# One encoder block on one Trainium2 core: 24 instead of 12 seven-product pairs in the down projection, weight sums made in the up projection

## What is computed

```python
n1 = rmsnorm(x, norm_mix_g)
proj = n1 @ w_in                      # 2048 -> 6152: mLSTM heads and RG-LRU blocks
x = x + mix @ w_out                   # 2048 x 2048
n2 = rmsnorm(x, norm_ffn_g)
gate, up = jnp.split(n2 @ w_up, 2, axis=-1)          # 2048 -> 2 x 5632
gate = causal_dwconv(gate, ffn_conv_w, ffn_conv_b)   # width 3
x = x + (jax.nn.silu(gate) * up) @ w_down            # 5632 -> 2048
return rmsnorm(x, norm_final_g)
```

## Time and profile before

| | |
|---|---|
| time, median of 3 runs | 1127.09 us (1127.08 to 1127.31) |
| span of the profiled execution | 1124.7 us; its own time is not listed apart from the three runs |
| busy: PE, weight loads | 1112.0 us (99%), 959.1 us (85%) |
| busy: DVE, ACT, POOL | 809.1 us (72%), 601.3 us (53%), 47.2 us (4%) |
| moved by DMA | 213.09 MB, mean 189 GB/s |
| mean granted TensorE clock | 0.997 of full speed |

### The profile page before, as it was taken

The page is one execution under the profiler, slowest core; times in us unless marked ns, Lnnn a source line. Parts: engine busy times, 40 slices in busy tenths (PEclk is TensorE's granted clock), DMA queues, the critical chain, the costliest instruction groups (busy, mean ns, idle before and its releaser), DMA issues.

```text
span 1124.7 us, 18049 instructions
## 1 busy us (share of the span) xinstructions
PE 1112.0 (99%) x5986; PEld 959.1 (85%) x5986; DVE 809.1 (72%) x1088; ACT 601.3 (53%) x818; POOL 47.2 (4%) x44
## 2 busy tenths in 40 slices
PE   9999999999999999999999999999999999999997
PEld 8888888888888888888888888888888888878886
DVE  6777586675775676776667667766766998689876
ACT  7656475564756554344444444444444666457553
POOL 0100000000000000000000000000000000000001
PEclk9999999999999999999999999999999999999999
DMA  8756657566565566656656665666566666556552
GB/s 256 234 166 192 178 147 231 151 186 186 198 202 173 175 198 190 185 172 211 196 168 187 206 189 164 207 199 191 158 214 191 221 228 219 170 168 217 196 183 78
DMA packets 166558, 213.09 MB, mean 189 GB/s; under 512 B 6988, under 2 KB 149584, under 8 KB 166400
## 3 DMA queue, kind: packets, MB, share of 16 engines
q1 hardware_dynamic: 165504, 210.40, 60.3%
q0 software_dynamic: 448, 1.78, 0.5%
q10 hardware_dynamic: 576, 0.53, 0.1%
HBM read 210.58 MB, written 2.10 MB: 189 GB/s over the span
## 4 chain that ended last, share of the span: by engine, by line
PE 95%; DVE 2%; ACT 1%; DMA 0%; issue 0%; DVEq 0%; ACTq 0%
PE ps L1305 42%; PE ps L1307 21%; PE ps L1440 21%; PE ps L1489 5%; PE ps L1302 2%; PE ps L1303 1%; PE ps L1288 1%; DVE w L721 1%; PE ps L1416 1%; ACT xn L411 0%; ACT w L411 0%; PE ps L1335 0%; DMA xres<-x_dram 0%; DVE xres L1038 0%; DVE s_w L1062 0%
## 5 line engine op out<-in xcount | busy, mean ns | idle before, releaser
L1305 PE MATMUL ps<-xT,w 128*128 128x512 f32 x2048 | 715.3, 395 | 0.0
L721 DVE TENSOR_TENSOR w<-raw,w 128x1024 fp32r<-128x1024 f32 x364 | 444.7, 1235 | 255.6 <-ACT w L411 254.8
L1307 PE MATMUL ps<-xT,w 128*128 128x256 f32 x2048 | 569.6, 278 | 0.0
L411 ACT ACTIVATE w<-raw 128x1024 fp32r<-128x1024 f32 (+2 forms) x373 | 384.8, 1045 | 336.7 <-PE ps L1307 242.1
L1305 PEld LDWEIGHTS ps<-xT,w 128*128 128x128 f32 x2048 | 384.1, 188 | 88.9
L1307 PEld LDWEIGHTS ps<-xT,w 128*128 128x128 f32 x2048 | 385.5, 188 | 0.3
L1440 PE MATMUL ps<-w,aT 128*128 128x512 f32 x1152 | 265.9, 391 | 2.5 <-DVE xres L1093 2.5
L1440 PEld LDWEIGHTS ps<-w,aT 128*128 128x128 f32 x1152 | 217.1, 189 | 48.0 <-DVE xres L1093 2.9
L411 ACT ACTIVATE fs<-fc 128x512 f32<-128x512 f32 x22 | 13.9, 632 | 101.4 <-DVE fc L1164 101.4
L1489 PE MATMUL ps<-s_w,s_act 128*128 128x512 f32 x252 | 59.2, 390 | 0.2 <-DVE xres L1038 0.2
L1489 PEld LDWEIGHTS ps<-s_w,s_act 128*128 128x128 f32 x252 | 47.2, 188 | 10.4 <-DVE xres L1038 0.7
(11 more groups left out here) (178 smaller groups left out, 577.5 us busy)
## 6 DMA issues: line engine op xcount, KB each, us to landing
raw<-w_up_dram SPq DMA_DIRECT2D x176, 512.0 KB, 4.6
raw<-w_in_dram SPq DMA_DIRECT2D x92, 512.0 KB, 3.9
raw<-w_down_dram SPq DMA_DIRECT2D x64, 512.0 KB, 4.4
raw<-w_out_dram SPq DMA_DIRECT2D x32, 512.0 KB, 4.5
s_raw<-w_down_dram SPq DMA_DIRECT2D x24, 512.0 KB, 4.9
raw<-w_in_dram SPq DMA_DIRECT2D x8, 256.0 KB, 7.0
xres<-x_dram SPq DMA_DIRECT2D x3, 512.0 KB, 7.3
y_dram<-xn SPq DMA_DIRECT2D x3, 384.0 KB, 3.2
```

The source lines that it names most:

```text
L411: return sc.activation(out_, in_, fn, **kw)
L721: v.tensor_tensor(w[:, s, :, 1, :], raw[:, s, :].rearrange("p (c n) -> p c n", c=CH), w[:, s, :, 0, :], ALU.subtract).then_inc(lo_ready, 1)
L1305: mm(full, w[:, s, c, 0, cut], xT[:, kt, :, :].rearrange("p a n -> p (a n)"), start=kt == 0, stop=False)
L1307: ins = mm(rest, w[:, s, c, 1, cut], xT[:, kt, 0, :], start=False, stop=kt == KT - 1)
```

## The change

Twelve pairs per half instead of six: four runs, each a body and three pairs, then one more body (five bodies instead of eight). The first and third pair of a run use `s_raw` and `s_w` (places `_x`), the second uses the ring's own `raw`, `w` and `aT`. The weight sums of all 24 pairs are made in the up projection: SP loads a pair's two K tiles (1 MB), DVE makes four sums in two steps between splits, SP stores them (1 MB) to device memory; the down projection loads them again. Activation tiles and their sums lie side by side, so a pair's activations are one operand of 896 columns. In half 0 the last body goes by slots. `pairs_out` is no longer spread over splits. `gfin` has lost its own buffer and is loaded into used slots of `act`.

```diff
-PERIODS = 6
-PERIOD = RING + 2
-DOWN_BODIES = (FT - 2 * PERIODS) // RING
+RUNS, RUN_PAIRS = 4, 3
+PAIRS = RUNS * RUN_PAIRS
...
+DOWN_BODIES = (FT - 2 * PAIRS) // RING
...
+SUMS_AT = (2, 8, 14, 20, 26, 32)
+SUMS_GAP = 6
...
+        pair_raw = s_raw[:], raw_flat
+        pair_w = s_w[:], w[:].rearrange("p s c a n -> p (s c a n)").rearrange("p (m a n) -> p m a n", m=S_WEIGHTS, a=2)
...
-                    sp.dma_start(s_raw[:, 2 * k:2 * k + 2, :].rearrange("p a n -> p (a n)"),
-                                 rows[bass.ds(b * PERIOD + (RING + k), 1), :, half * HALF:(half + 1) * HALF].rearrange("k p n -> p (k n)")).then_inc(s_landed, 16)
+                    src, dst = rows[:, bass.ds(first + s, 1), half * HALF:(half + 1) * HALF], raw[:, s, :].rearrange("p (b n) -> p b n", b=1)
+                    if pair_before is None:
+                        load(group, s, src, dst)
+                    else:
+                        sp.wait_ge(s_lo_ready, pair_before * S_PARTS + (1 if s < 2 else S_PARTS))
+                        sp.dma_start(dst, src).then_inc(raw_landed[s], 16)
...
+            def load_for_sums(run, q):
+                half, i = divmod(q, RUN_PAIRS)
+                src = down_rows[bass.ds(run * RUN_TILES + (RING + 2 * i), 2), :, half * HALF:(half + 1) * HALF]
+                sp.dma_start(s_raw[:, 0:2 * HALF].rearrange("p (k n) -> p k n", k=2), src.rearrange("k p n -> p k n")).then_inc(t_raw_landed, 16)
+            def store_sums(run, q):
+                t = run * len(SUMS_AT) + q
+                dst = sums_dram[bass.ds(t, 1)].rearrange("t p n -> p (t n)")
+                sp.wait_ge(t_summed, t * T_SUMS + T_SUMS)
+                sp.dma_start(dst, s_raw[:, 2 * HALF:4 * HALF]).then_inc(t_stored, 16)
...
+            def load_pair(half, run, i):
+                place, p = place_of(i), nth_pair(half, run, i)
+                cols = half * HALF
...
+                    sp.wait_ge(lo_ready, g * RING + (RING + 2))
+                elif i:
+                    sp.wait_ge(s_lo_ready, p * S_PARTS + (1 - 2 * S_PARTS))
+                elif half or not at_start(run):
+                    sp.wait_ge(s_lo_ready, p * S_PARTS + (1 - S_PARTS))
+                sp.dma_start(dst[:, 0:BANK], upper).then_inc(plain_landed[place], 16)
+                sp.dma_start(dst[:, BANK:BANK + HALF], lower).then_inc(plain_landed[place], 16)
+                if i == 1:
+                    sp.wait_ge(lo_ready, g * RING + 2 * RING)
+                elif i:
+                    sp.wait_ge(s_lo_ready, p * S_PARTS - S_PARTS)
+                elif half or not at_start(run):
+                    sp.wait_ge(s_lo_ready, p * S_PARTS)
+                sp.dma_start(dst[:, 2 * HALF:4 * HALF], sums).then_inc(sums_landed[place], 16)
             COL_Q, COL_K, COL_V, COL_O, COL_XR, COL_GR = 0, D_M, 2 * D_M, 3 * D_M, 4 * D_M + 2 * H, 4 * D_M + 2 * H + D_L
...
+                load_group(j * 2 + (G_UP + g), up_v, j * COLS + g * D_FF, ahead)
...
+            after(sp, A2, "std1")
+            with sp.Fori(0, RUNS) as run:
+                for it in range(RUN_ITERS):
+                    for g in range(2):
+                        def sums_of(s, unit=(2 * it + g) * RING):
+                            if unit + s - SUMS_GAP in SUMS_AT:
+                                store_sums(run, SUMS_AT.index(unit + s - SUMS_GAP))
+                            if unit + s in SUMS_AT:
+                                load_for_sums(run, SUMS_AT.index(unit + s))
+                        load_up(run * RUN_ITERS + (it + 1), g, sums_of)
+            for j in range(RUNS * RUN_ITERS + 1, UP_ITERS):
                 for g in range(2):
-                    load_group(j * 2 + (G_UP + g), up_v, j * COLS + g * D_FF)
+                    load_up(j, g)
...
+                load_pairs(half, 0)
+                with sp.Fori(1, RUNS) as run:
+                    load_body(run + g0, w_down, run * RUN_TILES, half, nth_pair(half, run, -2))
+                    load_pairs(half, run)
+                load_body(g0 + RUNS, w_down, RUNS * RUN_TILES, half, nth_pair(half, RUNS, -2))
+                for b in range(RUNS + 1, DOWN_BODIES):
                     load_body(g0 + b, w_down, FT + (b - DOWN_BODIES) * RING, half)
                 if half == 0:
-                    load_pair(1, 0)
                     load_body(g0 + DOWN_BODIES, w_down, 0, 1)
             for r in range(ROWS):
...
-            def prepare_body(src, group, first):
+            def prepare_body(src, group, first, pair_before=None):
                 for s in range(RING):
+                    if pair_before is not None:
+                        act_e.wait_ge(s_used, pair_before * S_STEPS + (1 if s < 2 else S_STEPS))
                     round_units(group, [s])
+                    if pair_before is not None:
+                        act_e.wait_ge(s_used, pair_before * S_STEPS + S_STEPS)
                     round_tiles(src, first, [s])
...
+                act_e.wait_ge(plain_landed[place], nth * S_LOADS + S_LOADS)
+                if i == 1:
+                    act_e.wait_ge(unit_used, g * RING + (RING + 2))
+                elif i:
+                    act_e.wait_ge(s_used, p * S_STEPS + (1 - 2 * S_STEPS))
+                elif half or not at_start(run):
+                    act_e.wait_ge(s_used, p * S_STEPS + (1 - S_STEPS))
...
+                if i == 1:
+                    act_e.wait_ge(unit_used, g * RING + 2 * RING)
+                elif i:
+                    act_e.wait_ge(s_used, p * S_STEPS - S_STEPS)
+                elif half or not at_start(run):
+                    act_e.wait_ge(s_used, p * S_STEPS)
+                act_fn(pair_act[place][:, 0, 0:A_COLS], pair_source(run, i)).then_inc(s_hi_ready, 1)
+                act_e.wait_ge(sums_landed[place], nth * 16 + 16)
+                for m in (T1, T2):
+                    act_fn(dst[:, m:m + 2, 0, :], src[:, m * BANK:(m + 2) * BANK].rearrange("p (m n) -> p m n", m=2)).then_inc(s_hi_ready, 1)
...
+                    def run_of_pairs(run):
+                        for i in range(RUN_PAIRS):
+                            pair_hi(half, run, i)
+                        if half == 1 and at_start(run):
+                            warm_sqrt(A4)
+                            for r in range(ROWS):
+                                squares(A4, r, 0, V4)
+                        prepare_body(act, run + (g0 + 1), run * RUN_SLOTS + RUN_SLOTS, nth_pair(half, run, RUN_PAIRS - 2))
+                    run_of_pairs(0)
+                    with act_e.Fori(1, RUNS) as run:
+                        run_of_pairs(run)
                     pairs_copy(half)
-                    prepare_body(act, g0 + DOWN_BODIES - 1, FT - RING)
+                    for b in range(RUNS + 1, DOWN_BODIES):
+                        prepare_body(act, g0 + b, ACT_SLOTS + (b - DOWN_BODIES) * RING)
                     if half == 0:
                         prepare_body(act, g0 + DOWN_BODIES, 0)
...
+                low(0, dst[:, 0:PLAIN, 1, :], src[:, 0:PLAIN * BANK].rearrange("p (m n) -> p m n", m=PLAIN), dst[:, 0:PLAIN, 0, :])
+                low(1, pair_act[place][:, 1, 0:A_COLS], pair_source(run, i), pair_act[place][:, 0, 0:A_COLS])
+                for n, m in ((2, T1), (3, T2)):
+                    low(n, dst[:, m:m + 2, 1, :], src[:, m * BANK:(m + 2) * BANK].rearrange("p (m n) -> p m n", m=2), dst[:, m:m + 2, 0, :])
...
-                did(v.tensor_tensor(xres[:, 0, first], bank_a, xres[:, 0, first], ALU.add), V4, f"xa{half}")
-                yield
-                did(v.tensor_tensor(total, bank_c, copy_a, ALU.add), V4, f"u{half}")
-                yield
+                did(v.tensor_tensor(xres[:, 1, second], bank_a, xres[:, 1, second], ALU.add), V4, f"xa{half}")
+                did(v.tensor_tensor(total, bank_c, total, ALU.add), V4, f"u{half}")
                 after(dve, V4, f"u{half}")
-                did(v.tensor_tensor(xres[:, 0, second], total, xres[:, 0, second], ALU.add), V4, f"xu{half}")
-                yield
+                did(v.tensor_tensor(xres[:, 1, first], total, xres[:, 1, first], ALU.add), V4, f"xu{half}")
                 did(v.tensor_tensor(total, bank_e, total, ALU.add), V4, f"z{half}")
-                yield
...
+                    def run_of_pairs(run):
+                        for i in range(RUN_PAIRS):
+                            pair_lo(half, run, i)
...
-                    split_body(act, g0 + 1, PERIOD, tiles + RING)
-                    with dve.Fori(1, PERIODS) as b:
-                        pair_lo(half, b)
-                        split_body(act, b + (g0 + 1), b * PERIOD + PERIOD, b * RING + (tiles + RING))
...
-                        split_units(g0 + DOWN_BODIES - 1, [s])
-                        split_tiles(act, FT - RING, tiles + (DOWN_BODIES - 1) * RING, [s])
-                        next(parts)
-                    for s in range(RING):
-                        if half == 0:
-                            split_units(g0 + DOWN_BODIES, [s])
```

(75 more changed lines are left out.)

208 lines of the change are left out of this document (97 added, 111 removed).

## The result

| | before | after |
|---|---|---|
| median of the runs | 1127.09 us | 1150.13 us (1147.57 to 1154.12) |
| ratio to before | | 1.021, 95% interval 1.0198 to 1.0222 |
| span of the profiled execution | 1124.7 us | 1145.7 us (its time 1147.57) |
| mean granted TensorE clock | 0.997 | 0.986 |
| matmuls on the two down lines | 1404 | 1368 |

What follows compares the result with a forecast made beforehand. TensorE was taken as the bound (busy 1112.0 of 1124.7 us). Terms -8.2 - 4.9 + 6.6 + 2.8 = -3.7 gave span 1121.0, time 1123.4 us; own range 1117 to 1129.6, whole range 1114 to 1133.

Steps and rivals of the forecast that it cites:

- 36 matmuls fewer: Down projection: twelve more pairs save 36 matmuls at 0.2267 us each, all on the path, -8.2 us.
- The change of halves: Down projection, between halves: the whole loss of idle and low clock is taken back, -4.9 us (bounds 0 and -4.9).
- The pairs in runs: Down projection: DVE's work and the transfers for each body and three pairs stay hidden behind TensorE, cost 0.
- the named thinnest place: Down projection, half 1: ACT's squares stand ahead of the second body's rounding; no cost was forecast.
- The five other sums: Up projection, sums at units 2, 8, 20, 26 and 32 of each run: no wait found, cost 0.
- The tail: Kernel's end: POOL's two products hold up DVE's two-SBUF-input steps, lengthening the uncovered end chain, +2.8 us (bounds 0 and 3.2).
- landed at 603.8: Up projection: unit 14's load lands behind a store and a sums load; TensorE waits 1.65 us per run, +6.6 us total.
- My upper bound: Up projection, wait at unit 14: 3.2 us per run if transfers move at 306 GB/s.
- The clock (B): Up projection: each of four waits lowers TensorE's clock, 8.5 us on top of the forecast, 1131.9 us; chance 0.16.
- A (the burst hides): Up projection: store and load overlap or slack is wider, so no wait; 1116.8 us; chance 0.27.
- C (the rate): Up projection turns transfer-bound: at 290 GB/s each run takes 4.8 us more, 1136 us; chance 0.11.
- D: Down projection: a pair waits on a late load or DVE, 1 us in each of eight runs, 1131.4 us; chance 0.10.

Runs made afterwards that it cites:

- the spread version: Against the kernel with three 1 MB buffers and late GpSimd tail products: 1 MB transfers spaced evenly, never two together; 1116.60 us.
- the first three-buffer kernel: Against the changed kernel: sums made in place in three 1 MB buffers in turn, loads, sums and stores at new units; 1131.77 us.
- the kernel with the early products: Against the changed kernel: GpSimd's two tail products wait for the low split of the last pair's weights, not the last pair on TensorE; 1150.91 us.

## Why the prediction was wrong

**Right.** 36 matmuls fewer, -8.2. The change of halves, -4.9: no gap, clock 1.00. The pairs in runs: 0, but for 0.9 us at the named thinnest place (0.56 idle and a body of 11.19). The five other sums: 0, shown by leaving out the sixth. The tail: 2.8 forecast, 3.5 in the trace, with some luck: I let only `xu` wait for POOL, but of the 3.1 us by which DVE was held, 2.2 stand at aT's last split, which I had not counted, and 0.9 at `xu`. The kernel with no transfers in the up projection ran in 1117.65 us, where these terms give 1116.8.

**The step that failed** is "landed at 603.8" in the part on the sums: place and kind of the wait were right, its size was not. From the store's issue to the landing of unit 14's load I had 9.1 us; the trace has 439.64 to 451.83, 12.2. I had put 2.0 us around the data and 7.1 for it: store, load and unit load, 2.62 MB, at a mean of 369 GB/s (401 and 353). The same stretch of the trace, without its first 1.1 and its last 0.9 us, is 440.74 to 450.93; the view of its transfers, and below it that of its first 3.2 us:

```profile
DMA packets 1717, 3.39 MB, mean 332 GB/s; under 512 B 73, under 2 KB 1333, under 8 KB 1589
```

```profile
DMA packets 333, 1.15 MB, mean 364 GB/s; under 512 B 16, under 2 KB 218, under 8 KB 218
```

The packet sizes tell the transfers apart: the store's are 8 KB (128), those of the raw tiles' load 4 KB (256), those of unit loads 1 KB (512 each). So in 10.2 us 3.39 MB moved at 332 GB/s, and two things make up the missing 3.1 us. The larger is traffic that the sum left out: 0.77 MB of other unit loads, 2.3 us at that rate. About 0.2 MB of it is in the first 3.2 us, beside 115 packets of the store: unit 13's load was still in flight, and ACT's round that waits for it starts at 443.80. The rest comes later, when the loads of the units behind 14 moved beside 14's own: being issued first did not give a load the engines to itself. The smaller is the rate: 2.62 MB at 332 and not 369 GB/s, 0.8 us. So 1.65 + 3.1 = 4.75 us of idle against 4.65 measured, 12 us more over four runs. My upper bound, 3.2 us, held a lower rate and left out all traffic but the three transfers.

**The rival that came on top.** The clock (B) was priced at 2.12 us per stop, 8.5 in all, at a chance of 0.16; it cost 8.7. I had tied it to the length of the wait. With the longer waits both happened. By the spans, 1121.0 + 12.0 + 8.7 + 0.9 + 0.7 = 1143.3, against 1145.7; 2.4 us stay unassigned, 1.7 of them in the up projection. (The profiled execution ran 1147.57 us, 1.9 and not 2.4 over its span; the median lies 2.6 above it.) The two were not rivals but one event: who prices a stop of TensorE must price the clock behind it in the same case, and my range did not. The price itself was read a little high: the 2.12 us behind the stop of the earlier trace rows hold its later wait of 0.25 us too.

**The other rivals.** A (the burst hides) fell for this kernel, but is what the spread version does. C (the rate) fell: the same 33.5 MB per run pass without a stop if they are spread. D came to 0.9 of its 8 us. One slip had no effect: a pair's transfers are 1.84 MB, so a run of three takes 7.6 MB and 302 GB/s, not 7.4 and 294.

## What to carry to other kernels

A transfer added to a queue is priced at the tightest load behind it, not at the average share: here 20 of 24 pairs of a store and a load were free and four cost 27 us. Count all bytes that move until the load has landed, those in flight before the burst and those issued behind the load too, and use the rate of a mixed stretch, not the best stream of the trace. To hide the bytes, give the new transfers buffers of their own and place them one by one, away from loads that must land ahead of a serial step; another queue didn't help here, since it shares the engines.

## What was not expected of the hardware

- **The clock after a stop is not a matter of its length alone.** In all kernels here the stops of 3.5 to 4.8 us were followed by a clock of 0.62 to 0.82 over the next 8 us. But without the stores, a stop of 1.93 us was followed by 0.79 and one of 3.16 us by 1.00 (table by windows behind both restarts):

```profile
463.15:471.15 8.00, 8.00 (x46) 7.00 (x47) 7.65 (x8) 3.91 (x5) 0.00 (x0) 1.00 0.81 251
576.28:584.28 8.00, 8.00 (x37) 6.96 (x38) 7.01 (x7) 3.43 (x5) 0.00 (x0) 0.79 0.80 251
```

- **A slower pace at full clock after some stops.** Behind many of the stops, short and long, the pairs of matmuls came 0.353 us apart instead of 0.347, some 2% slower, for tens to hundreds of microseconds, until one of the next stops. No trace without a stop in the up projection has it. The same 30 us with the transfers only and without the burst at 14:

```profile
470.00:500.00 30.00, 30.00 (x171) 26.03 (x170) 20.37 (x26) 13.93 (x16) 1.29 (x1) 1.00 0.90 289
```

```profile
470.00:500.00 30.00, 30.00 (x175) 26.22 (x174) 25.36 (x38) 11.65 (x14) 1.30 (x1) 1.00 0.92 295
```

Both have a clock of 1.00 and no idle time, and 171 against 175 matmuls. It explains most of why 6.4 us of stops cost the first three-buffer kernel some 13 us against the spread one (1131.77 less 1.9 for the tail, against 1116.60): in the traces its up projection is 14.4 us longer, 6.4 of it idle, some 6.2 the pace (about 330 us of it slow), and 1.8 open. The changed kernel's trace has none of this pace; the kernel with the early products, whose up projection is the same, has it from about 590 to 821 us, behind a stop of 4.60 us. That may be part of why the changed kernel's executions spread from 1147.57, the profiled one, to 1154.12, but no run shows it. The cause of the pace wasn't tried and stays open.
